# Even layer: roots of the head norms and the gate scans' argument are kept in PSUM banks

## The reference

```
q = _rmsnorm(q.reshape(bsz, L, A_HEADS, A_HEAD_DIM), q_norm)     # 8 heads of 64
k = _rmsnorm(k.reshape(bsz, L, A_HEADS, A_HEAD_DIM), k_norm)
o_a = _dsa_attention(q, k_all, v_all, qi, wi, ki_all, ...)       # top-k keys, softmax
log_alpha = log_sigmoid(ab @ gate_w2 + gate_b2) / 16
b = jnp.cumsum(gc, axis=-2)                                      # gc = log_alpha of a chunk of 64
o = (qc * exp(b)) @ S + causal((qc*exp(b - b_mid)) (kc*exp(b_mid - b))) @ vc
out = concat([o_a, o_b]) @ w_out
```

## Time and profile before

| | us |
|---|---|
| median of 3 runs | 1477.51 |
| lowest and highest | 1476.26, 1480.02 |
| profiled execution, device time | 1478.12 |
| its span, first to last instruction | 1476.4 |
| TensorE busy | 1423.6 |
| VectorE busy | 896.6 |
| ScalarE busy | 597.5 |
| GpSimd busy | 370.6 |

### The profile page before, as it was taken

The page is one execution under the profiler, slowest core; times in us unless marked ns, Lnnn a source line. Parts: engine busy times, 40 slices in busy tenths (PEclk is TensorE's granted clock), DMA queues, the critical chain, the costliest instruction groups (busy, mean ns, idle before and its releaser), DMA issues.

```text
span 1476.4 us, 25253 instructions
## 1 busy us (share of the span) xinstructions
PE 1423.6 (96%) x9708; PEld 1389.8 (94%) x9708; DVE 896.6 (61%) x1403; ACT 597.5 (40%) x975; POOL 370.6 (25%) x344
## 2 busy tenths in 40 slices
PE   7999999999779999999999999999999889999998
PEld 7999999999658999999999999989999779999998
DVE  5666655678755666655666655667565456666542
ACT  5333324446443433332433332558433544333322
POOL 4000024766415100012100003637766232000000
PEclk9999999999789999999999999989999999999999
DMA  7655951344202555864455684122222222555751
GB/s 186 179 158 146 285 146 42 116 129 139 87 3 87 143 144 157 210 178 97 123 158 145 167 228 117 58 86 87 59 85 58 90 85 82 155 157 147 185 149 44
DMA packets 324028, 188.23 MB, mean 127 GB/s; under 512 B 10954, under 2 KB 321352, under 8 KB 323964
## 3 DMA queue, kind: packets, MB, share of 16 engines
q1 hardware_dynamic: 322080, 183.22, 45.0%
q0 software_dynamic: 1216, 3.98, 0.9%
q10 hardware_dynamic: 668, 0.15, 0.1%
HBM read 183.22 MB, written 4.11 MB: 127 GB/s over the span
## 4 chain that ended last, share of the span: by engine, by line
PE 89%; DVE 6%; ACT 3%; issue 1%; DMA 1%; SPq 0%; ACTq 0%
PE PS L620 21%; PE PS L621 21%; PE PS L622 21%; PE PS L725 2%; PE PS L726 2%; PE PS L727 2%; PE PS L1193 2%; PE PS L1176 2%; PE PS L746 1%; PE PS L748 1%; PE PS L747 1%; PE PS L698 1%; PE PS L699 1%; PE PS L700 1%; DVE RA L2099 1%
## 5 line engine op out<-in xcount | busy, mean ns | idle before, releaser
L620 PE MATMUL PS<-h_hi,w_parts 128*128 128x320 f32 x1408 | 438.2, 311 | 7.1 <-DVE h_lo L1907 4.1
L621 PE MATMUL PS<-h_lo,w_parts 128*128 128x320 f32 x1408 | 436.4, 310 | 0.0
L622 PE MATMUL PS<-h_hi,w_parts 128*128 128x320 f32 x1408 | 436.3, 310 | 0.0
L620 PEld LDWEIGHTS PS<-h_hi,w_parts 128*128 128x128 f32 x1408 | 265.5, 189 | 8.8 <-issue 7.4
L621 PEld LDWEIGHTS PS<-h_lo,w_parts 128*128 128x128 f32 x1408 | 265.5, 189 | 0.3
L622 PEld LDWEIGHTS PS<-h_hi,w_parts 128*128 128x128 f32 x1408 | 265.4, 189 | 0.0
L1339 ACT ACTIVATE w_parts<-gu 128x1024 fp32r<-128x1024 f32 x176 | 176.6, 1050 | 158.4 <-PE PS L622 154.8
L620 PE MATMUL PS<-act_hi,w_parts 128*128 128x320 f32 x704 | 217.7, 309 | 0.0
L622 PE MATMUL PS<-act_hi,w_parts 128*128 128x320 f32 x704 | 217.6, 309 | 0.0
L621 PE MATMUL PS<-act_lo,w_parts 128*128 128x320 f32 x704 | 217.6, 309 | 0.0
L1895 DVE TENSOR_TENSOR w_parts<-gu,w_parts 128x1024 fp32r<-128x1024 f32 x176 | 209.1, 1229 | 3.4 <-ACT w_parts L1339 3.3
(11 more groups left out here) (386 smaller groups left out, 2380.5 us busy)
## 6 DMA issues: line engine op xcount, KB each, us to landing
gu<-in_ffn_w_gate SPq DMA_DIRECT2D x88, 512.0 KB, 4.0
gu<-in_ffn_w_up SPq DMA_DIRECT2D x88, 512.0 KB, 5.2
dn<-in_ffn_w_down SPq DMA_DIRECT2D x32, 1408.0 KB, 7.0
gu<-in_od_w_in SPq DMA_DIRECT2D x32, 512.0 KB, 5.0
gu<-in_ev_w_in SPq DMA_DIRECT2D x26, 512.0 KB, 4.8
dn<-in_ev_w_out SPq DMA_DIRECT2D x4, 1024.0 KB, 6.3
dn<-in_od_w_out SPq DMA_DIRECT2D x4, 1024.0 KB, 5.4
RB<-bias_rows POOLq DMA_DIRECT2D x2, 576.0 KB, 6.1
```

Source lines behind the costliest of these rows:

```text
L620: mm(out, w_hi, hi, start=first, stop=False)
L621: mm(out, w_hi, lo, start=False, stop=False)
L622: return mm(out, w_lo, hi, start=False, stop=last)
```

## The change

The reciprocal roots of the query and key head norms are no longer written to `rs` and `k_rstd`, but over their own sums in banks 4 to 7, and VectorE's products read them from there. The log-sigmoid (L2117) is written to banks 4 and 5 and the scans read it from there. Three waits of TensorE follow the banks' new use: the key head sums wait for the query products (`q_ready` 8), the gate's product for the key products (`k_ready` 4), and `scores(0)` for the end of the gate's differences (`g_args`).

```diff
-        k_rstd = dn[:, 1, 1280:2560].rearrange("p (a t) -> p a t", a=4)
@@ even(), TensorE
                     if l == 9:
-                        head_sums(4, s["qk_read"], 1)
+                        head_sums(4, s["q_ready"], 8)
@@ gate()
-                pe.wait_ge(s["qk_read"], 2)
+                pe.wait_ge(s["k_ready"], 4)
@@ scores(0)
-                        pe.wait_ge(s["gate_used"], 1)
+                        pe.wait_ge(s["g_args"], 1)
@@ ScalarE
-                        rsqrt(view(rs, 0, 4, T), banks(4, 4, T), 1.0 / A_D, (s["qk_read"], 1)).then_inc(s["qk_rstd"], 1)
+                        rsqrt(banks(4, 4, T), banks(4, 4, T), 1.0 / A_D, (s["qk_read"], 1)).then_inc(s["qk_rstd"], 1)
-                        rsqrt(k_rstd, banks(4, 4, T), 1.0 / A_D, (s["qk_read"], 2)).then_inc(s["qk_rstd"], 1)
+                        rsqrt(banks(4, 4, T), banks(4, 4, T), 1.0 / A_D, (s["qk_read"], 2)).then_inc(s["qk_rstd"], 1)
@@ VectorE
                         ins = stt(qbd[h, :, p, par * CH:(par + 1) * CH],
                                   pr[h, T_Q + p, :].rearrange("p (c t) -> p c t", t=CH)[:, :, ::-1], cols[h, C_QN:C_QN + 1],
-                                  rs[h, p * T:(p + 1) * T].rearrange("p (c t) -> p c t", t=CH)[:, :, ::-1], ALU.mult, ALU.mult)
+                                  bank(4 + p, T)[h, :].rearrange("p (c t) -> p c t", t=CH)[:, :, ::-1], ALU.mult, ALU.mult)
-                    stt(pr[:, T_K + p, :], pr[:, T_K + p, :], cols[:, C_KN:C_KN + 1], k_rstd[:, p, :],
+                    stt(pr[:, T_K + p, :], pr[:, T_K + p, :], cols[:, C_KN:C_KN + 1], bank(4 + p, T),
                         ALU.mult, ALU.mult).then_inc(s["k_ready"], 1)
-                link(stt(gx, gx, 0.0, gx2, ALU.min, ALU.subtract))
+                link(stt(banks(4, 2, T), gx, 0.0, gx2, ALU.min, ALU.subtract))
-                        ins = ve.tensor_tensor_scan(gB[:, p, w], ones[:, 0:CH], gx[:, p, w], 0.0, ALU.mult, ALU.add)
+                        ins = ve.tensor_tensor_scan(gB[:, p, w], ones[:, 0:CH], bank(4 + p, T)[:, w], 0.0, ALU.mult, ALU.add)
```

## The result

The changed kernel takes 1481.65 us in the median (1480.19 to 1482.79, 10 runs) against 1477.26 (1476.26 to 1480.02, 10 runs) for the kernel before: ratio 1.0027, 95% interval 1.0019 to 1.0035. By the ratio that is +4.0 us (the medians lie 4.4 apart), where +0.5 was forecast. The profiled execution took 1482.4 us, its span is 1480.7.

A forecast was written before the change was run, and what follows sets the result against it. The even layer was taken as bound by TensorE up to 371.4, then VectorE's gate chain, then a mixture with TensorE's clock. Profiled 1478.1 plus 0.5 gave 1478.6, the median lying 0.6 lower: forecast 1478.0, range 1472 to 1484.

The forecast's parts named there:

- the likeliest of the three outcomes: Whole kernel: time within about 0.3%, 4.4 us, of no change, chance 0.70, against faster 0.14 and slower 0.16.
- (1): Query products: eight read from a bank take 3.8 us (3.3 to 4.4), ending at 338.6, not 346.0.
- (2): Key head sums: TensorE waits for the query products and stands 4.4 us, in a stage without slack.
- (3): Behind the pause before the key head sums: TensorE at half clock for a while, 1.6 us lost (0 to 3.2).
- (4): Key products and gate(): products take 1.9 us instead of 5.99, TensorE waits 1.2 us more (0.9 to 1.5).
- (5): Loads 12 and 13 end 7.2 us later (4.8 to 9.7), and the log-sigmoid starts 3.5 us later.
- (6): Gate chain: scans take 1.9 us, not 6.1, a GpSimd collision adds 1.3; g_args at 376.2 against 376.33.
- (7): Scores wait for g_args: logits +0.95, a GpSimd turn +0.7, faster clock -1.1, so +0.5 us at 395.
- (a): Scores and value-row turns behind g_args: at half clock they take 10 us, not 5; about 1483.5, chance 0.15.
- (b): No clock fall after the first pause, no GpSimd collision, full clock from 385 to 395; about 1473, chance 0.12.
- (d): Products with a bank operand still take turns with GpSimd, g_args some 12 us later; 1489, chance 0.03.
- (c): TensorE's pauses cost nothing and only VectorE's gains count: -5 to -7 us, about 1472, chance 0.05.

The follow-up runs named there:

- e10: Kernel before with one wait changed, the key head sums wait for the query products (q_ready 8), all operands in SBUF; 1.0027, +4.0 us.
- e1: Changed kernel with the gate's part undone: roots stay in banks, log-sigmoid in SBUF, scores(0) waits for gate_used; 1.0008, +1.2 us against the kernel before.
- e3: Kernel before with only the query roots in banks and the key head sums waiting for q_ready 8; 0.9987, -1.9 us.
- e4: Changed kernel with GpSimd's product of 1280 columns held until the gated keys and queries are done (bds_ready 3); 1.0046, +6.8 us against the kernel before.
- e2: Kernel before with the gate's part alone: log-sigmoid in banks 4 and 5, scans from there, scores(0) waits for g_args; 0.9998.
- e5: Changed kernel with the key roots back in SBUF and gate() waiting for their read only; 1.0001 against the kernel before.
- e9: Changed kernel with GpSimd's bias sums held for g_args and its product of 1280 columns for p_ready 3; 1.0003 against the kernel before.
- e6: Kernel before, operands in SBUF, GpSimd's two bias sums held for g_args and its product of 1280 columns for p_ready 3; 0.9963, -5.5 us.
- e7: Roots in banks, head sums, key roots and gate() behind loads 10, 11 and 12, scans in SBUF, GpSimd held; 0.9989, -1.6 us against the kernel before.

## Why the forecast was right, and where its size was off

The range, 1472 to 1484, held, and so did the likeliest of the three outcomes, within 0.3%, but by little: the ratio says 0.27%, and its interval, 0.19 to 0.35%, reaches across the line. It also leaves out no change: the loss is real, where the forecast expected none that could be told. The size of the shift did not hold. By the steps:

(1) The operand works as said, but eight query products took 4.60 us, not 3.8, beyond the bound of 4.4: they start 0.58 apart. The undisturbed ones of e10, from SBUF, start 0.58 apart too (341.53, 342.12, 342.69), so the bank adds nothing. The four key products, read in plain direction, do start 0.46 apart (357.27 to 358.65); that the reversed reading of the queries makes the difference was not tried. The Trainium skill's 62 cycles more for a PSUM source ("VectorE: DVE Perf Modes", section "The TRN2 errata") don't show either: 542 to 551 ns from SBUF (these three) and 540 to 554 from the bank, ten scans 1.94 and 1.89.

(2) and (3) Pause 4.97 us for 4.4. The head sums at half clock took 3.97 us instead of 2.56 (0.24 of it a wait), **1.4** for 1.6.

(4) The pause before gate() is 1.18 us for 1.2. But a second stretch at half clock follows it: gate() to load 13's end takes 1.5 us more (e1 against e3). The sum had allowed the clock to fall only once. By the Trainium skill's "TensorE: Matmul & The Clock Gate", section "Part 1: The HAM clock gate", the half clock is the default that activity lifts; the trace agrees with the direction, after a pause of only 1.18 us, but behind the later pause of 2.23 us the granted clock stayed at 1.00.

(5) So load 13 ends 9.7 us later, the upper bound of the step, not 7.2, and the log-sigmoid 5.8 instead of 3.5.

(6) The gate chain came out as worked out: 0.83, 1.89 and 0.82 us, and the collision at L2125 of 1.07. The differences end +2.0, where the sum had -0.1; the difference is what (1) to (4) missed.

(7) is the step that failed. Logits behind the scores: +1.3 for +0.95, but this term was not on the path at all. In e4, where nothing holds the negation, ACT's first softmax exponent (45.85 us after the first query product) starts as its own gate exponents end (45.94), not as the negation ends (45.53). Its 0.95 us in the sum made up by luck for part of what the sum lacked. Then I put GpSimd's third piece on the key products L2134 at a quarter of its length, 0.7 us. It fell on the negation L2195, whose operands I had not looked at: 2.23 us, right before the value on which ACT waits. ACT's slack of 1.7 us (before, its gate exponents ended that much after the negation) took part of it: from +5.6 to +3.9. And the 1.1 us that a faster clock was to bring back did not come: scores and value rows did run at full clock, but key turns to updates take 10.0 us, before 9.83, since the clock falls again at 388.05. In the prediction's own terms, -0.1 + 0.95 + 0.7 - 1.1 became 2.0 + 0 + 1.9 + 0.2: 4.1 us at the end of the updates.

Rival (a) did not happen in its place (378.62 to 388.05 at 1.00), (b) and (d) not at all. But (a)'s fall of the clock did come in two other kernels with the third wait: behind e2's pause of 8.09 us (373.96 to 384.00 at 0.72), and within the scores and turns behind e5's, which was 2.23 us long as in the changed kernel:

```profile
376.50:380.50 4.00, 4.00 (x20) 3.91 (x19) 3.90 (x5) 2.18 (x10) 2.88 (x2) 0.57 0.98 335
```

So the length of a pause alone doesn't tell whether the clock falls behind it. The prediction's argument against (a), that TensorE is dense before the pause, holds for e5 as well; that (a) stayed away here is in part luck. Rival (c) fails: in e10 a pause of 8.8 us moves load 13's end by 10.9 us and the time by 4.0.

What gained and what lost, by parts added: query roots -1.9 us (e3); key roots on top +3.1 (e1 against e3); the gate's part on top +2.8 (the whole against e1), the last two with e1's mixture in them. By parts taken from the whole: without the key part -3.8 (e5), without the gate's part -2.8 (e1), with GpSimd held -3.5 (e9). The last three sum to far more than 4.0: the parts don't add up, and undoing any one of them removes most of the loss. These differences have intervals of 1.3 to 1.9 us either way. How the loss divides between (2), (3) and (4) is read from traces; that the clock costs the 1.5 us rests on two stretches of the same work, not on a run in which only the clock differs.

## What to carry to other kernels

Where VectorE and GpSimd take turns, first ask whether GpSimd's work can wait: holding two sums and a product back brought 0.37% with two waits, and moving operands into banks lost 0.27%: a bank that is read longer makes TensorE wait, and what is placed behind TensorE's work moves with it. A hold has to end where VectorE has operations with a PSUM operand or is idle (e9, e6), not just "later" (e4). And in a sum, allow for a fall of the clock behind every pause of TensorE, as a range and not as a fixed price: behind 1.18 us before gate() it fell in all five traces with that pause, behind 2.23 us before the scores in one of three, behind 2.31 us in e7 not. Look at every small operation of VectorE between two waits, not at the large ones alone. And compare several executions of each kernel before dividing a difference of a few us: a granted clock that differs behind the part in question can be worth as much.

## What the runs showed of the hardware

- A VectorE operation with a single SBUF input can wait for GpSimd too, if it is a TENSOR_SCALAR from SBUF to SBUF: 128x4 elements, 0.17 us alone, took 2.40 beside GpSimd's product. Beside GpSimd's work TENSOR_REDUCE (0.42), MAX8 (0.76) and operations with a PSUM operand (0.42, 0.55) kept their length. The Trainium skill, "SBUF — State Buffer", section "Who interferes with whom", names `tensor_scalar` among the operations that can contend with GpSimd; I had not applied it to an operation this small.
- Turns are whole instructions: in e4 a product of VectorE that started 0.10 us behind GpSimd's took 3.35 us, and in e10 the query products and GpSimd's splits alternate at 1.5 us.
- Pauses of 1.18 and 4.97 us of TensorE in the projections were each followed by a stretch at 1.2 GHz (e1's second one cost 1.5 us). Pauses of 2.23 us before the scores (changed kernel, e4), of 1.16 there in e9 and of 2.31 in e7 were not; the same 2.23 us in e5 was.
- The same 50 small products of TensorE, key turns to updates, took from 6.4 us (granted clock 1.00, e9) to 10.5 us (0.53, e10).
- ACT's Exp and Ln of 1280 elements in place in a bank took 1.22 and 1.30 us; before, Exp within SBUF took 1.27 and Ln from bank to SBUF 1.33.
